# Routing, down bias and first gather of a top-4-of-32 mixture-of-experts step, rearranged ahead of the expert loop

## The reference

```python
mod = silu(c) @ w_ada + b_ada                  # shift, scale, gate twice
u = x * (1 + scale1) + shift1
proj = u @ w_in                                # conv, pooling and gate branches
h = layer_norm(ALPHA * x + gate1 * (merged @ w_o))
v = h * (1 + scale2) + shift2
logits = v @ w_router + b_router               # 32 experts
gates = softmax(top4(logits))
# for each chosen expert e, up to 64 of its tokens at a time here:
hh = v_e @ w_up[e] + b_up[e]                   # 1024 x 2048
act = min(glu, 7) * sigmoid(1.702 * glu) * (clip(lin, -7, 7) + 1)
f += gate * (act @ w_down[e] + b_down[e])      # 1024 x 1024
y = layer_norm(ALPHA * h + gate2 * f)
```

## Time and profile before

| | |
|---|---|
| profiled execution | 1328.42 us, of which the span of the profile 1326.6 us |
| median of 3 runs | 1329.97 us |
| granted TensorE clock, mean | 0.955 |
| PE busy | 1218.2 us (92%) |
| DVE, ACT, POOL busy | 564.0, 230.1, 149.4 us |
| DMA | 466.45 MB, mean 352 GB/s |
| first expert matmul of round 0 | 311.92 us |

### The profile page before, as it was taken

One profiled execution on the slowest core, in us unless ns is written; L12 is line 12 of the kernel. 1 busy time (PEld: TensorE's weight loads), 2 busy tenths in 40 slices (PEclk: granted clock), 3 DMA queues, 4 the chain that ended last, 5 costly groups with the idle time before them and its releaser, 6 DMA issues.

```text
span 1326.6 us, 17547 instructions
## 1 busy us (share of the span) xinstructions
PE 1218.2 (92%) x6199; PEld 523.0 (39%) x6200; DVE 564.0 (43%) x1062; ACT 230.1 (17%) x355; POOL 149.4 (11%) x90
## 2 busy tenths in 40 slices
PE   3899999867999999999989999999999999999980
PEld 0599964432333333333333333333333333333320
DVE  0617735865334343334334334343343433434346
ACT  0232200241111111111111111121111111111111
POOL 0367352074000000000000000000000000000003
PEclk8799999957999999999999999999999999999995
DMA  9744498645999999999996999998799999699941
GB/s 337 250 168 153 191 347 331 267 163 201 427 426 425 426 427 427 426 427 426 426 424 249 429 427 423 426 427 374 318 426 428 426 427 426 260 421 426 427 188 40
DMA packets 54708, 466.45 MB, mean 352 GB/s; under 512 B 5467, under 2 KB 5499, under 8 KB 18561
## 3 DMA queue, kind: packets, MB, share of 16 engines
q1 hardware_dynamic: 52817, 460.36, 84.2%
q0 software_dynamic: 1872, 5.84, 1.3%
HBM read 464.33 MB, written 1.85 MB: 351 GB/s over the span
## 4 chain that ended last, share of the span: by engine, by line
PE 66%; DMA 23%; DVE 7%; ACT 2%; issue 1%; SPq 1%; DVEq 0%; POOL 0%; ACTq 0%
PE bank L853 30%; DMA ring<-in_w_up 17%; PE bank L886 14%; PE bank L623 7%; PE bank L826 4%; PE bank L743 3%; DMA ring<-in_w_ada 3%; DMA hx<-in_x_sample 2%; PE bank L609 1%; PE bank L877 1%; ACT front L1016 1%; DMA mod_rows<-parts_home 1%; PE bank L845 1%; PE bank L782 1%; PE bank L811 1%
## 5 line engine op out<-in xcount | busy, mean ns | idle before, releaser
L853 PE MATMUL bank<-ring,front 128*64 128x512 f32 x2240 | 508.0, 599 | 14.9 <-DMA ring<-in_w_up 14.7
L853 PEld LDWEIGHTS bank<-ring,front 128*64 128x64 f32 x2240 | 151.2, 137 | 315.3 <-issue 285.1
L886 PE MATMUL bank<-ring,front 128*64 128x512 f32 x1120 | 248.0, 595 | 7.3 <-ACT front L1016 7.3
L1303 DVE TENSOR_TENSOR front<-front,bank 128x512 f32<-128x512 f32 (+1 forms) x210 | 143.6, 684 | 85.9 <-PE bank L826 73.2
L886 PEld LDWEIGHTS bank<-ring,front 128*64 128x64 f32 x1120 | 77.3, 137 | 153.8 <-issue 139.9
L1347 DVE TENSOR_TENSOR O_low<-bank,O_high 128x512 fp32r<-128x512 f32 x35 | 24.2, 691 | 244.3 <-ACT O_high L1019 244.3
L1013 ACT ACTIVATE front<-front 128x256 f32<-128x256 f32 x70 | 29.1, 416 | 546.4 <-DVE front L1321 546.4
L534 POOL TENSOR_TENSOR parts_home<-parts_home,front 128x1024 f32<-128x1024 f32 x2 | 4.7, 2373 | 992.1 <-ACT parts_home L948 992.1
L1321 DVE TENSOR_SCALAR front<-bank 128x256 f32<-128x256 f32 x70 | 29.7, 424 | 155.3 <-PE bank L853 154.1
L455 POOL TENSOR_TENSOR ring_parts<-ring,ring_parts 128x1024 fp32r<-128x1024 f32 x28 | 68.3, 2469 | 77.6 <-ACT ring_parts L919 77.6
L743 PE MATMUL bank<-parts_home,front 128*64 128x512 bf16 (+1 forms) x576 | 74.3, 389 | 0.0
(11 more groups left out here) (217 smaller groups left out, 961.7 us busy)
## 6 DMA issues: line engine op xcount, KB each, us to landing
ring<-in_w_up SPq DMA_DIRECT2D x128, 2048.0 KB, 17.4
ring<-in_w_down SPq DMA_DIRECT2D x128, 1024.0 KB, 16.8
ring<-in_w_ada SPq DMA_DIRECT2D x12, 2048.0 KB, 16.8
ring<-in_w_in SPq DMA_DIRECT2D x8, 2048.0 KB, 13.3
ring<-in_w_o SPq DMA_DIRECT2D x2, 2048.0 KB, 19.0
hx<-in_x_prompt SPq DMA_DIRECT2D x2, 1024.0 KB, 23.0
ring<-in_w_out_a SPq DMA_DIRECT2D x1, 2048.0 KB, 7.7
ring<-in_w_out_b SPq DMA_DIRECT2D x1, 2048.0 KB, 15.1
```

The lines of the kernel that those rows point to most:

```text
L853: last = mm(bank[B_UP[j]][64 * h:64 * h + 64, :], x_T[:, (c % 2) * 2 + b, 64 * (c // 2):64 * (c // 2) + 64], w[:, :, at:at + 256], start=F ...
L886: last = mm(bank[B_DOWN][64 * h:64 * h + 64, :], act_T[:, 2 * j + b, 64 * hh:64 * hh + 64], expert_chunk_at(UP_CHUNKS + m)[:, b * 1024 + h ...
L1303: signal(TT(Y[0:r, 2 * t + h, :], Y[0:r, 2 * t + h, :], bank[b][0:r, :], ALU.add), bank_free[b], value)
```

## The change

1. The masks and small tables of the routing are bf16: `mask`, `rounds`, `passed` and the constants `tri`, `ones`, `tri_incl`. The mask is made by one comparison for all four places (`chosen`) and one sum.
2. Ranks are kept one higher, 0 for a token that isn't there; the rank is one instruction, and the constants for slots move by one (`rank_of_slot`).
3. V is computed by DVE from the residual rows, without ACT's normalised rows; ACT still writes those for the end of the kernel.
4. The six `bias` matmuls and their six copies go. Instead O_high, O_low and onehot_T hold b_down and the gates in two parts each when round 0 starts, and round 0's combine adds the bias. Y is cleared by POOL. The gate rows are copied four times (128 partitions) instead of three.
5. The first gather works in fp32, from V itself and a one-hot `S_first`, behind the table and the transposes. It needs no parts of V.
6. Three first parts of V are made by ACT before round 0; the other six, and POOL's six remainders, after the first gather, and `gather` of round 0 (for round 1) waits for all nine.
7. PE's loop no longer waits for `route_ready` at its start; `token_rows` is behind the first combine, and waits there. On DVE `add_up` of tile 0 goes ahead of `hot` and `weighed`. B_X and B_T change banks.

The diff, cut:

```diff
+        rank_of_slot = const[:, C_IOTA + 1:C_IOTA + 1 + NT]
+        const16 = const[:, C_BF:C_N].bitcast(BF16)
+        tri = const16[:, BF_TRI:BF_TRI + P]
+        tri_twice = const16[:, BF_TRI2:BF_TRI2 + P]
+        ones = const16[:, BF_ONE:BF_ONE + P]
+        tri_incl = const16[:, BF_TRI1:BF_TRI1 + E]
...
+            wait_full(pool, "o11")
+            for i in range(4):
+                pool.dma_start(b_down_raw[32 * i:32 * i + E, :], a["b_down"][0][:, (i // 2) * 512:(i // 2 + 1) * 512]).then_inc(b_down_landed, 16)
+            pool.wait_ge(v_ready, 3)
+            pool.memset(onehot_T[:, :].bitcast(F32), 0.0).then_inc(cleared, 1)
+            pool.memset(O_low[:, :].bitcast(F32), 0.0).then_inc(cleared, 1)
+            pool.wait_ge(rank_rows_ready, 1)
+            pool.memset(Y, 0.0).then_inc(cleared, 1)
+            pool.wait_ge(bank_full[B_X], front_uses(B_X) + 1)
+            pool.wait_ge(route_ready, 1)
+            pool.wait_ge(O_low_ready, 1)
+            for t, q in RESTS:
...
-            def gather(n, x_rows_read=None):
-                pe.wait_ge(S_ready, n + 1)
-                if x_rows_read is not None:
-                    pe.wait_ge(x_rows_ready, x_rows_read)
+            def gather(n, x_rows_read):
+                pe.wait_ge(S_ready, n)
+                pe.wait_ge(v_part_ready, len(PARTS))
+                pe.wait_ge(x_rows_ready, x_rows_read)
...
-            def bias(pieces):
-                for i in pieces:
-                    t, h = divmod(i, 2)
-                    ps = take(f"bias{i}")
-                    done(f"bias{i}", mm(ps[0:ROWS[t], :], route_T[0:E, 1, t * P:t * P + ROWS[t]], b_down_rows[0:E, h, :],
-                                        start=True, stop=True))
-            pe.wait_ge(softmax_ready, 1)
-            route_transposes("gate_T", 1)
-            wait_read(pe, "gate_T")
-            pe.wait_ge(b_down_landed, 16)
-            bias((0, 1, 2))
             pe.wait_ge(rounds_ready, 1)
             ps = take("bounds")
             done("bounds", mm(ps[0:E, 0:1], tri_incl[0:E, :], rounds[0:E, :], start=True, stop=True))
-            bias((3, 4, 5))
+            pe.wait_ge(softmax_ready, 1)
+            route_transposes("gate_T", 1)
             pe.wait_ge(passed_ready, 1)
             ps = take("table")
             mm(ps[0:1, 0:NROUND], ones[0:E, 0:1], passed[0:E, :], start=True, stop=True)
             mm(ps[0:1, NROUND:2 * NROUND], rounds[0:E, :], passed[0:E, :], start=True, stop=True)
             done("table", mm(ps[0:1, 2 * NROUND:2 * NROUND + E], rounds[0:E, :], tri_incl[0:E, :], start=True, stop=True))
+            pe.wait_ge(rank_rows_ready, 1)
             route_transposes("rank_T", 0)
-            for b in (B_X, B_XT):
-                wait_read(pe, FRONT[[n for n in range(len(FRONT)) if n % 8 == b][-1]])
-            pe.wait_ge(v_part_ready, len(PARTS))
-            gather(0)
+            wait_read(pe, FRONT[[n for n in range(len(FRONT)) if n % 8 == B_X][-1]])
+            pe.wait_ge(S_first_ready, 1)
+            for t in range(3):
+                for h in range(2):
+                    last = mm(bank[B_X][64 * h:64 * h + 64, :], S_first[0:ROWS[t], t, :], V[0:ROWS[t], t, h * 512:(h + 1) * 512],
+                              start=t == 0, stop=t == 2)
+            last.then_inc(bank_full[B_X], 1)
+            wait_read(pe, FRONT[[n for n in range(len(FRONT)) if n % 8 == B_XT][-1]])
             x_transposes(0)
             def token_rows(n):
...
+                pe.wait_ge(route_ready, 1)
...
-            pe.wait_ge(route_ready, 1)
...
+                    if c == 0:
+                        token_rows(g)
...
+            for t, q in PARTS[:3]:
...
+            act.wait_ge(b_down_landed, 64)
+            AF(O_high[:, :], b_down_raw[:, :], ACT.Copy).then_inc(O_high_ready, 1)
+            ps = wait_full(act, "gate_T")
+            act.wait_ge(cleared, 1)
+            AF(onehot_T[:, 0:NT], ps[:, 0:NT], ACT.Copy).then_inc(gate_high_ready, 1)
             route_copy("gate_T", 1)
-            for i in range(6):
-                ps = wait_full(act, f"bias{i}")
-                r = ROWS[i // 2]
-                free(f"bias{i}", AF(Y[0:r, i, :], ps[0:r, :], ACT.Copy))
             route_copy("rank_T", 0)
             x_copy(0)
             xT_copy(0)
+            for t, q in PARTS[3:]:
+                part_of_v(t, q)
...
-                dve.wait_ge(row_normed, i + 1)
-                step(TT(V[0:r, t, :], hx[0:r, t, :], vec[:, 2, :], ALU.mult))
-                signal(TT(V[0:r, t, :], V[0:r, t, :], vec[:, 1, :], ALU.add), v_ready, i + 1)
+                row = V[0:r, t, :]
+                normalise(r, meanwhile=lambda: step(STT(row, hx[0:r, t, :], aggr[0:r, 0:1], vec[:, 2, :], ALU.subtract, ALU.mult)))
+                signal(STT(row, row, rstd[0:r, :], vec[:, 1, :], ALU.mult, ALU.add), v_ready, i + 1)
...
-                step(v.tensor_copy(top_f[0:r, t, :], top_index[0:r, t, :]))
+                if t == 2:
+                    step(v.tensor_copy(L[NS_TOK:P, t, :], L[0:NS_TOK, t, :]))
+                step(v.max(top[:, t, :], L[:, t, :]))
+                step(v.max_index(top_index[:, t, :], top[:, t, :], L[:, t, :]))
             by_e = lambda t: t.to_broadcast([P, 3, E])
-            experts = iota[:, 0:E].unsqueeze(1).to_broadcast([P, 3, E])
             signal(TT(eq, L, by_e(top[:, :, 0:1]), ALU.subtract), logit_ready, 1)
-            step(TT(mask, experts, by_e(top_f[:, :, 0:1]), ALU.is_equal))
+            step(v.tensor_copy(top_f, top_index[:, :, :]))
+            experts = iota[:, 0:E].unsqueeze(1).unsqueeze(1).to_broadcast([P, 3, TOPK, E])
+            step(TT(chosen, experts, top_f[:, :, 0:TOPK].unsqueeze(3).to_broadcast([P, 3, TOPK, E]), ALU.is_equal))
+            with nc.allow_low_precision(reason="sums of one-hots that are 0 or 1"):
+                signal(v.reduce_sum(mask, chosen.rearrange("p t k e -> p t e k"), AX_X), mask_ready, 1)
             dve.wait_ge(exp_ready, 1)
-            for k in range(1, TOPK):
-                step(TT(eq, experts, by_e(top_f[:, :, k:k + 1]), ALU.is_equal))
-                ins = TT(mask, mask, eq, ALU.add)
...
-            step(v.memset(rank, -1.0))
-            for t in range(3):
-                r = ROWS[t]
-                ins = STT(rank[0:r, t, :], ps[0:r, t * E:(t + 1) * E], 1.0, mask[0:r, t, :], ALU.add, ALU.mult)
-                step(ins) if t < 2 else free("rank", ins)
-            for t in range(3):
-                step(TS(rank[0:ROWS[t], t, :], rank[0:ROWS[t], t, :], -1.0, None, ALU.add))
-            step(v.tensor_copy(rank[NS_TOK:P, 2, :], rank[0:NS_TOK, 2, :]))
-            step(v.tensor_copy(copies(0), each_copy(rank)))
+            free("rank", STT(rank, ps[:, 0:3 * E].rearrange("p (t e) -> p t e", t=3), 1.0, mask, ALU.add, ALU.mult))
+            first_slots = rank_of_slot[:, 0:SLOTS].unsqueeze(1).to_broadcast([P, 3, SLOTS])
+            signal(TT(S_first, first_slots, by_slot(rank[:, :, 0:1]), ALU.is_equal), S_first_ready, 1)
             ps = wait_full(dve, "bounds")
             free("bounds", v.tensor_copy(bound[0:E, :], ps[0:E, 0:1]))
             signal(TS(passed[0:E, :], iota[0:E, 0:NROUND], bound[0:E, :], None, ALU.is_ge), passed_ready, 1)
-            one_hots(0, 0, 0)
+            signal(v.tensor_copy(copies(0), each_copy(rank)), rank_rows_ready, 1)
...
+            dve.wait_ge(gate_high_ready, 1)
+            for at in (32, 96):
+                low, raw = onehot_T[at:at + E, 0:NT], route_T[at:at + E, 1, :]
+                high = onehot_T[at:at + E, 0:NT].bitcast(F32)
+                step(TT(low, raw, high, ALU.subtract)) if at == 32 else signal(TT(low, raw, high, ALU.subtract), onehot_ready, 1)
...
+            dve.wait_ge(cleared, 3)
+            dve.wait_ge(O_high_ready, 1)
+            for at in (0, 64):
+                low, raw, high = O_low[at:at + E, :], b_down_raw[at:at + E, :], O_high[at:at + E, :].bitcast(F32)
+                step(TT(low, raw, high, ALU.subtract)) if at == 0 else signal(TT(low, raw, high, ALU.subtract), O_low_ready, 1)
...
+                add_up(g, 0)
                 dve.wait_ge(bank_full[B_T], g * 2 + front_uses(B_T) + 1)
                 step(TT(hot, bank[B_T][:, 0:NT], slot_of_row[:, bass.ds(now, 1)].to_broadcast([P, NT]), ALU.is_equal))
                 dve.wait_ge(bank_full[B_XT], g * 2 + front_uses(B_XT) + 2)
                 step(STT(weighed, bank[B_XT][:, 0:NT], 1.0, hot, ALU.mult, ALU.mult, accum_out=slot_gate))
-                add_up(g, 0)
```

133 lines of the change are left out of this document (61 added, 72 removed).

## The result

The kernel after takes 1308.78 us (median of 4 runs, 1306.94 to 1310.79), the one before 1329.48 (4 runs, 1328.73 to 1330.07): ratio 0.9845, 95% interval 0.9828 to 0.9862. The forecast was 1310.0 in a range of 1303 to 1317. The profiled execution of after took 1310.79 us, the longest of the four, with a span of 1309.0.

A forecast was written before the change was run, and what follows sets the result against it. Until 700 us the weight stream was taken to set the time, starting once PE has used chunk 0 of round 0. A front 26.0 us earlier plus 7 for row loads gave -19.0, so 1310 us; range 1303 to 1317.

The forecast's parts named there:

- V: End of V's computation on DVE: ready at 264.2 us instead of 266.58, -2.4 us.
- Logits and top 8: Routing up to subtracting the maximum: the index cast no longer waits for POOL's subtracts; -6.7 us so far.
- Mask: Routing mask from a cast, a comparison and a sum over 384 elements: ready at 272.15, -9.3 us so far.
- Rank to gather: From rank to the first gather's end, without bias matmuls and with an fp32 gather of 5.2 us: -19.9 us so far.
- To round 0: From the first gather to the first expert matmul, the wait for gate and rank parts moved behind: -26.0 us so far.
- Parts of V in round 0: V's remaining parts, made during round 0, are ready at 301.6, before PE's gather at 304.2: no wait.
- Row loads: POOL's 2.89 MB of norm and end rows now fall into the weight stream: +7 us taken, 0 to 8.1 possible.
- In the loop: PE's loop with token_rows and add_up moved: 0 taken, between -0.05 and +0.05 us a round.
- loads cost nothing: Rival: the row loads run beside the weight stream for free, so -26 us, 1304; chance 0.11.
- Round 0 is held up: Rival: POOL's subtracts and passes over hx hold DVE in rounds 0 and 1, about +6 us, 1316; chance 0.14.
- The loop gets longer: Rival: add_up ahead of `hot` makes PE wait at each second combine; at 1.3 us a round, 1337; chance 0.04.
- The early start isn't reached: Rival: an unseen wait keeps chunk 0 of round 0 within a few us of 317.8, so 1328; chance 0.03.

The follow-up runs named there:

- e1: The changed kernel with POOL's row loads and passes over hx held until expert 13's and expert 20's weights have landed: 1302.55 us.
- e3: The changed kernel with the 1.84 MB of rows for the end of the kernel loaded twice: 1317.29 us.
- e4: The changed kernel with eight extra copies on ACT ahead of the first copy of x_T, holding back the start: 1315.9 us.
- e9: The changed kernel with V computed again from ACT's normalised rows, in the order of the kernel before: 1310.78 us.
- e6: The changed kernel with five extra subtractions on POOL when V is ready, beside the routing: 1312.65 us.
- b3: The kernel before, with POOL's row loads and passes over hx held until the 14th and 21st experts' weights have landed: 1326.17 us.
- b1: The kernel before without the down bias (six matmuls and six copies left out): 1329.1 us.
- e5: The changed kernel with token_rows and its wait ahead of chunk 0 again, as before: 1311.86 us.
- e2: The changed kernel without POOL's nine passes over hx, the loads kept: 1309.33 us.
- e8: e1 with PE's load of the count of rounds moved ahead of the first transposes: 1303.09 us.
- b2: b3 also without the down bias (its six matmuls and six copies left out): 1319.33 us.
- e10: e1 with POOL's passes over hx held three experts longer, until the 17th expert's weights have landed: 1304.86 us.

## Why the prediction was right

The mechanism was right: an earlier start of the stream, less what the row loads cost in it. The total came within 1.2 us of the median, and that closely by luck: the loads cost 2.4 more than taken and the steps of the front gave 0.9 less, against which stand 0.9 of chance ahead of the change, 0.9 in chunk 0 and a spread of 3.9 us between after's runs.

| step of the forecast | forecast | measured | net of 0.9 |
|---|---|---|---|
| V ready | -2.4 | -2.93 | -2.05 |
| mask | -9.3 | -9.49 | -8.6 |
| gather ends | -19.9 | -19.99 | -19.1 |
| first expert matmul | -26.0 | -26.03 | -25.15 |
| chunk 0 | 0 | -0.89 | |
| row loads in the stream | +7 | +9.4 | |
| loop | 0 | -0.1 | |

Net of 0.9: everything ahead of the change ran 0.8 to 0.9 us earlier in the profile of after (its modulation rows came at 229.12 instead of 229.90), which is chance.

- *What bounds the kernel.* e1, e3 and e4 bear it out. The parts of the 17.9 us add up to 18.2 (the trace has 17.8), which changes nothing. But the matmuls don't lead all the way from 699.94: before's chain waits for weights again at 891.19 and 1110.86.
- *V.* The fused passes take 1.28 us and not 1.23. e9 has V 2.1 later.
- *Logits and top 8.* That subtracts on POOL hold this cast is shown by e6, which holds it in the changed kernel (2.31 us for 24 indices); b3 shows that the passes over hx are not what held it. That the 7.45 us of before end with POOL's third subtract is read from the ends, there and in b1 to b3. The Trainium skill ("SBUF — State Buffer", Who interferes with whom) lets a cast in a two-port mode contend with GpSimd for as long as the other's instruction lasts; the trace agrees for one instruction, but this cast began beside the end of one subtract and waited through three more in a row, 6.28 us (and e6's through one, 2.31).
- *Mask.* The sum over 384 elements took 0.81 us; I took 0.56 from a range of 0.26 to 0.9.
- *Rank to gather.* The bf16 counts were as taken (0.46 for the ranks' six records). The gather at the lower clock took 5.29; 5.2 was taken. By before and b1, 8.3 us of the 12.0 gained ahead of it are the bias; the other 3.7 (bf16 counts, fewer instructions on DVE) no run takes apart.
- *To round 0.* 3.64 us as forecast. 5.0 of the 6.0 gained are POOL's passes no longer beside the parts of gates and ranks (b3).
- *Parts of V in round 0.* POOL 287.25 to 300.01, ACT's last part to 301.10, the gather at 303.02: no wait, as forecast.
- *Row loads.* The mis-sized term: 9.2 to 9.4 where +7 was taken and 8.1 was the upper bound. By the rates beside e3 most of the excess lies where the rows for the end run. The Trainium skill ("Trainium Kernel Development and Optimization", Key Constraints) says that such transfers share the 16 engines; e1 agrees that they are not free. By bytes alone they would be 6.8.
- *In the loop.* 0 was taken, within 0.05 us either way, and a round other than 27.3 us was to be a sign against the forecast. It is 27.15, by the moved token_rows (e5). The end doesn't show it (-0.1), since PE only waits longer for the weights behind the first doubled expert: 4.3 us in all against 2.0.

Of the rivals, "loads cost nothing" fell by e1. "Round 0 is held up" did not happen in after's profile, where round 1 lost 7 us of PE instead, all covered (e2). It did in e6, e8 and e9, whose gather and chunk 0 ran at the higher clock, and cost something only in e8, which has no row loads in the stream. "The loop gets longer" fell: the period of PE's rounds is 27.15 us against 27.30. "The early start isn't reached" fell by the first issue at 291.07.

The median fell by 20.7 us, the profiled span by 17.6, and the sum said 19.0; the spread of after's four runs (3.9 us) covers both. The executions here differ by the clock in the gather, the bias rows and chunk 0, worth 2.9 us ahead of the first issue in e6 and e9.

## What to carry to other kernels

Find the first moment from which a saturated stream runs, and measure every edit as (moment of its start) + (bytes in it): here 26.9 us earlier and 9.4 us longer. Transfers that can wait for a gap of the stream should: two waits gave 6 us on top of the rewrite's 21. Before costing an edit in the front, take the next wait in line away too; b1 alone would have said that eleven microseconds of matmuls were worth nothing. And where two resources take turns, a saving in one (0.15 us a round of PE here) shows only in the stretches that it bounds.

## What the runs showed of the hardware

- Small rows that POOL loads into all partitions cost a saturated stream more than their bytes: 3.2 us per MB for both together (9.2 us for 2.89 MB, e1) and 3.85 for a second load of the end rows (e3), against 2.36 for weights. While the end rows run, all queues together move 305 to 326 GB/s with the engines' busy share at 1.00.
- POOL's memset of Y, 2.66 us, held a DVE instruction of 64 elements for 2.24 us, though the two touch different data (0.18 us without it in b2). PE didn't wait for it, but DVE's work behind it and POOL's subtracts at 287.25, which wait for O_low, came 2 us later:

```profile
276.52 2.24 DVE L1278 TENSOR_SCALAR table<-front 1x64 int32<-1x64 f32 x1
```

- The same gather and the same first chunk took 4.11 to 4.18 and 3.60 us in e6, e8 and e9, and 5.07 to 5.32 and 4.83 to 5.02 in after, e1, e2, e3 and e10. The instructions are the same; the granted clock differs. So a mask that is 4.2 us later can come out as a first issue 1.3 later (e9).
